# Five of twelve blocks of x transposed by VectorE and GpSimd's transfers, no longer by TensorE

## What is computed

```python
x = x + 0.5 * swiglu(rmsnorm(x, ffn1_norm), ffn1_wg, ffn1_wu, ffn1_wd)   # 2048 -> 5632 -> 2048
x = x + hybrid_mixer(rmsnorm(x, mix_norm), w_in, ..., w_out, cos, sin)   # short convolution and sparse attention
x = x + 0.5 * swiglu(rmsnorm(x, ffn2_norm), ffn2_wg, ffn2_wu, ffn2_wd)
return rmsnorm(x, final_norm)

def rmsnorm(x, g):
    return x * lax.rsqrt(jnp.mean(x * x, axis=-1, keepdims=True) + EPS) * g
```

## Time and profile before

| | |
|---|---|
| median of 3 executions | 1814.29 us |
| span of the profiled execution | 1810.6 us |
| TensorE busy | 1799.3 us, 99% |
| VectorE busy | 1555.0 us, 86% |
| ScalarE busy | 1022.7 us, 56% |
| GpSimd busy | 246.2 us, 14% |
| chain that ended last | PE 93%, DVE 5%, ACT 1%, DMA 1% |

### The profile page before, as it was taken

How to read it: one execution, slowest core, us unless ns; L and a number is a source line. 1 busy time by engine, 2 the same in 40 slices (tenths; PEclk the granted TensorE clock), 3 DMA queues, 4 the chain that set the end, 5 groups by cost and what they waited for, 6 DMA issues and landing times.

```text
span 1810.6 us, 21958 instructions
## 1 busy us (share of the span) xinstructions
PE 1799.3 (99%) x8134; PEld 1481.8 (82%) x8134; DVE 1555.0 (86%) x1863; ACT 1022.7 (56%) x1334; POOL 246.2 (14%) x442
## 2 busy tenths in 40 slices
PE   9999999999999999999999999999999999999998
PEld 7788888888888888888788888888888888888886
DVE  7999998889999977678667867899999889999987
ACT  6655555445555556556567745555555455555554
POOL 1111111001111100000123300111111000222100
PEclk9999999999999999999999999999999999999999
DMA  7676766667676766766443655667676666677764
GB/s 244 209 213 221 217 210 211 207 202 220 206 216 203 218 201 207 209 214 194 149 138 107 209 174 185 209 207 218 209 216 212 214 207 194 209 219 221 242 202 151
DMA packets 199289, 367.28 MB, mean 203 GB/s; under 512 B 19013, under 2 KB 23857, under 8 KB 199057
## 3 DMA queue, kind: packets, MB, share of 16 engines
q1 hardware_dynamic: 185008, 352.37, 62.5%
q0 software_dynamic: 11648, 12.02, 2.2%
q10 hardware_dynamic: 2528, 1.52, 0.3%
HBM read 350.11 MB, written 4.19 MB: 196 GB/s over the span
## 4 chain that ended last, share of the span: by engine, by line
PE 93%; DVE 5%; ACT 1%; DMA 1%; issue 0%; ACTq 0%; DVEq 0%
PE ps L771 23%; PE ps L773 23%; PE ps L772 23%; PE ps L789 7%; PE ps L791 7%; PE ps L790 7%; PE ps L838 2%; DVE w_lo L1820 2%; DVE wt_lo L1892 1%; DVE wt L1882 0%; ACT w_hi L1305 0%; PE ps L1069 0%; PE ps L1096 0%; DMA raw<-in_ffn_wu_dram 0%; PE ps L1071 0%
## 5 line engine op out<-in xcount | busy, mean ns | idle before, releaser
L1820 DVE TENSOR_TENSOR w_lo<-raw,w_hi 128x1024 fp32r<-128x1024 f32 x573 | 692.1, 1225 | 111.8 <-ACT w_hi L1305 107.8
L1305 ACT ACTIVATE w_hi<-raw 128x1024 fp32r<-128x1024 f32 x573 | 599.6, 1056 | 287.3 <-PE ps L773 197.8
L771 PE MATMUL ps<-w_hi,hT_hi 128*128 128x512 f32 x1308 | 512.4, 392 | 1.3 <-ACT gu L1399 1.2
L773 PE MATMUL ps<-w_hi,hT_lo 128*128 128x512 f32 x1308 | 509.6, 390 | 0.0
L772 PE MATMUL ps<-w_lo,hT_hi 128*128 128x512 f32 x1308 | 509.3, 389 | 0.0
L712 POOL DMA_DIRECT2D gu_raw<-gu_sq x352 | 187.5, 541 | 1077.2 <-DVE gu_sq L2066 1003.7
L1356 ACT ACTIVATE wt_hi<-wt 128x1024 fp32r<-128x1024 f32 x164 | 172.9, 1054 | 274.7 <-DVE wt L1882 274.7
L771 PEld LDWEIGHTS ps<-w_hi,hT_hi 128*128 128x128 f32 x1308 | 245.7, 188 | 52.0 <-ACT gu L1399 2.1
L773 PEld LDWEIGHTS ps<-w_hi,hT_lo 128*128 128x128 f32 x1308 | 245.6, 188 | 52.0
L772 PEld LDWEIGHTS ps<-w_lo,hT_hi 128*128 128x128 f32 x1308 | 245.7, 188 | 49.7
L1892 DVE TENSOR_TENSOR wt_lo<-wt,wt_hi 128x1024 fp32r<-128x1024 f32 x164 | 199.6, 1217 | 0.0
(11 more groups left out here) (312 smaller groups left out, 2219.6 us busy)
## 6 DMA issues: line engine op xcount, KB each, us to landing
raw<-in_ffn_wu_dram SPq DMA_DIRECT2D x176, 512.0 KB, 4.5
raw<-in_ffn_wd_dram SPq DMA_DIRECT2D x176, 512.0 KB, 4.8
raw<-in_ffn_wg_dram SPq DMA_DIRECT2D x175, 512.0 KB, 4.1
raw<-in_w_in_dram SPq DMA_DIRECT2D x88, 512.0 KB, 3.6
raw<-in_w_out_dram SPq DMA_DIRECT2D x32, 512.0 KB, 4.2
gu_raw<-gu_sq POOLq DMA_DIRECT2D x352, 32.0 KB, 3.5
x_parked<-x SPq DMA_DIRECT2D x8, 256.0 KB, 5.3
raw<-in_cmp_k_w_dram SPq DMA_DIRECT2D x8, 256.0 KB, 3.2
```

Of the source, the lines that this page charges most:

```text
L771: mm(o, x_hi, w_hi[:, s, kk, :], start=begin, stop=False, skip_group_check=skip)
L773: ins = mm(o, x_lo, w_hi[:, s, kk, :], start=False, stop=last and kk == GK - 1, skip_group_check=skip)
L1305: act.activation(w_hi[:, c % SLOTS, :, :], raw[:, c % SLOTS, :, :], ACT.Copy).then_inc(hi_ready, 1)
L1820: tt(w_lo[:, s, :, :], raw[:, s, :, :], w_hi[:, s, :, :].bitcast(F32), ALU.subtract).then_inc(lo_ready, 1)
```

## The change

Blocks (1, 0), (1, 1), (2, 0), (2, 1) and (2, 2), `CARRIED` in this order, take the squares' path; the other seven stay on TensorE. `x_turn` is DVE's squares of x, `x_blocks` POOL's 16 transfers, `moved_operand` the four scaled copies on ACT and the four on DVE, which now read `gu_raw` in SBUF. Four semaphores are new: `x_squares` (turned), `x_moved` (landed, 256 a block), `x_moved_hi`, `x_moved_lo`. As `gu_sq` is single, DVE's next `x_turn` waits for the last block's landing; as `gu_raw` is single, POOL's next transfers wait for DVE's copies of the last block.

```diff
+def turned_by_pe(which, n):
+    return which == 0 or n == NDC - 1 or which == 1 and n == NDC - 2
+CARRIED = [(which, n) for which in (1, 2) for n in range(NDC) if not turned_by_pe(which, n)]
+CARRY_AT = {0: (23, 27, 28), 1: (28, 32, 33)}
...
+            def x_blocks(which, n):
+                u = CARRIED.index((which, n))
+                pool.wait_ge(x_squares, u + 1)
+                if u:
+                    pool.wait_ge(x_moved_lo, u)
+                for a_ in range(QB):
+                    for c_ in range(QB):
+                        pool.dma_start(gu_raw[c_ * SQ:c_ * SQ + SQ, :, a_, :],
+                                       gu_sq[a_ * SQ:a_ * SQ + SQ, :, c_ * P:c_ * P + P]).then_inc(x_moved, 16)
...
             ffn(0)
+            for n in CARRY_AT:
+                x_blocks(1, n)
...
+            for n in range(NDC - 1):
+                x_blocks(2, n)
             ffn(1)
...
             def x_operand(which, j):
-                pe.wait_ge(free[4 + j % 2], operand_use(which, j % 2, j // 2) + 1)
+                if turned_by_pe(which, j // 2):
+                    pe.wait_ge(free[4 + j % 2], operand_use(which, j % 2, j // 2) + 1)
+                else:
+                    pe.wait_ge(x_moved_lo, CARRIED.index((which, j // 2)) + 1)
...
-                        if f == 0 and part == 1 and g in (X0_AT, len(order) - 1):
-                            x_transposes(1, int(g > X0_AT))
...
-                for n in range(NDC - 1):
-                    put(AT[("out", NDC + n + 1), 1], lambda n=n: x_transposes(2, n))
...
+            def moved_operand(which, n):
+                vec0 = (V_FFN1, V_MIX, V_FFN2)[which]
+                act.wait_ge(x_moved, 16 * QB * QB * (CARRIED.index((which, n)) + 1))
+                for kk in range(QB):
+                    k = QB * n + kk
+                    ins = act.activation(hT_hi[:, k, :].rearrange("p (g s) -> p g s", s=SQ),
+                                         gu_raw[:, :, :, kk * SQ:kk * SQ + SQ].rearrange("p t a s -> p (t a) s"),
+                                         ACT.Copy, scale=vecs[:, vec0 + k:vec0 + k + 1])
+                ins.then_inc(x_moved_hi, 1)
...
-                            if f == 0 and g == X0_AT + 4:
-                                x_operand(1, 0)
+                            for n, steps_ in CARRY_AT.items():
+                                if f == 0 and g == steps_[1]:
+                                    moved_operand(1, n)
...
                 for n in range(NDC - 1):
-                    put(AT[("out", NDC + n + 1), 3], lambda n=n: x_operand(2, n))
+                    if n < NDC - 2:
+                        put(AT[("out", NDC + n + 2), 2], lambda n=n: moved_operand(2, n))
...
+            def x_turn(which, n):
+                u = CARRIED.index((which, n))
+                dve.wait_ge(resid_done, resid((None, R_FFN1B, R_ATT)[which], n))
+                if u:
+                    dve.wait_ge(x_moved, 16 * QB * QB * u)
+                for t in range(NT):
+                    ins = nc.vector.transpose(gu_sq[:, t, :].rearrange("p (c k s) -> p c k s", c=QB, s=SQ),
+                                              x[:, t, n * CH:n * CH + CH].rearrange("p (k c s) -> p c k s", c=QB, s=SQ))
+                ins.then_inc(x_squares, 1)
...
+                    put(done("out", NDC + n) + 1, lambda n=n: x_turn(2, n))
+                    if n < NDC - 2:
+                        put(AT[("out", NDC + n + 2), 3], lambda n=n: moved_operand(2, n))
```

More of the change, by code:

```diff
@@ L156 @@
 R_FFN1B, R_CONV, R_ATT, R_FFN2B = range(4)
+def turned_by_pe(which, n):
+    return which == 0 or n == NDC - 1 or which == 1 and n == NDC - 2
+CARRIED = [(which, n) for which in (1, 2) for n in range(NDC) if not turned_by_pe(which, n)]
+TURNED = [(which, n) for which in range(2) for n in range(NDC) if turned_by_pe(which, n)]
+CARRY_AT = {0: (23, 27, 28), 1: (28, 32, 33)}
 def resid(stage, n):
@@ L278, in mixer_banks @@
     uses += [(("cb", 0), 6), (("cb", 1), 7), (("css",), 6), (("ass",), 7)]
-    first = {4: 2 * NDC, 5: 2 * NDC, 6: 0, 7: 0}
+    first = {4: len(TURNED), 5: len(TURNED), 6: 0, 7: 0}
     seen, table = dict(first), {}
@@ L498, in build_program @@
         gu_moving = sem("gu_moving")
+        x_squares = sem("x_squares")
+        x_moved = sem("x_moved")
+        x_moved_hi = sem("x_moved_hi")
+        x_moved_lo = sem("x_moved_lo")
         gu_moved = sem("gu_moved")
@@ L846, in x_transposes @@
                     pe.wait_ge(resid_done, resid(R_FFN1B if which == 1 else R_ATT, n))
-                    if which == 1 and n < 2:
-                        pe.wait_ge(prod_free, job_no(0, ("down", 1, n)) + 1)
+                    if which == 1:
+                        pe.wait_ge(prod_free, job_no(0, ("down", 1, 1)) + 1)
                 for b in range(2):
@@ L1855, in x_operand, with moved_operand @@
                 for b in range(2) if b is None else (b,):
-                    scaled_operand(hT_hi, hT_lo, 4 * n + 2 * b, vec0, (4 + b,), OP_X[which] + 2 * n + b)
+                    at_ = len(TURNED) if which == 2 else TURNED.index((which, n))
+                    scaled_operand(hT_hi, hT_lo, 4 * n + 2 * b, vec0, (4 + b,), 2 * at_ + b)
+            def x_turn(which, n):
[7 more added lines that the diff above has]
+                ins.then_inc(x_squares, 1)
+            def moved_operand(which, n):
+                vec0 = (V_FFN1, V_MIX, V_FFN2)[which]
+                dve.wait_ge(x_moved_hi, CARRIED.index((which, n)) + 1)
+                for kk in range(QB):
+                    k = QB * n + kk
+                    split = lambda u: u[:, k, :].rearrange("p (g s) -> p g s", s=SQ)
+                    ins = stt(out=split(hT_lo), in0=gu_raw[:, :, :, kk * SQ:kk * SQ + SQ].rearrange("p t a s -> p (t a) s"),
+                              scalar=vecs[:, vec0 + k:vec0 + k + 1], in1=split(hT_hi).bitcast(F32),
+                              op0=ALU.mult, op1=ALU.subtract)
+                ins.then_inc(x_moved_lo, 1)
             def variance(phase, width, ssq_count, cols=NDC):
@@ L1917, in h_sums @@
                 if step == 0:
-                    for b in range(2):
-                        dve.wait_ge(free[4 + b], operand_use(2 if f else 0, b, 1) + 1)
+                    if f:
+                        dve.wait_ge(x_moved_lo, CARRIED.index((2, 1)) + 1)
+                    else:
+                        for b in range(2):
+                            dve.wait_ge(free[4 + b], operand_use(0, b, 1) + 1)
                     pick = lambda buf: buf[:, k0:k0 + 2 * quads, :].rearrange("p (q r) t -> p q r t", q=quads)
@@ L2169, in down @@
                                 residual(1, FFN0[f] + down_slot(1, 1), 1, half)
-                            if f == 0 and g == X0_AT + 4:
-                                x_operand(1, 0)
+                            for n, steps_ in CARRY_AT.items():
+                                if f == 0 and g == steps_[2]:
+                                    moved_operand(1, n)
+                                if f == 0 and g == steps_[0]:
+                                    x_turn(1, n)
                             if f == 1 and g in (23, 25, 39):
```

18 lines of the change are left out of this document (6 added, 12 removed).

## The result

The changed kernel takes 1838.74 us (median; 1837.36 to 1840.3), the kernel before beside it 1814.13 (1812.19 to 1815.16): ratio 1.0137, 95% interval 1.0125 to 1.0149, 24.6 us slower. The spans of the profiled executions differ by 1835.6 - 1810.6 = 25.0 us, and that is what follows explains. (Medians of the kernel before in later comparisons are 1813.5 to 1814.7.)

What follows compares the result with a forecast made beforehand. TensorE's list of matmuls was taken as the bound. Waits of 4.7 + 5.9 + 14.8 = 25.4 less 4.5 saved gave +20.9 on a span of 1810.6, 1831.5; with 3.7 for the runs' median, 1835 us, range 1825 to 1846.

Steps and rivals of the forecast that it cites:

- What is removed, 4.5 us: Five blocks of eight transposes leave TensorE's list, 0.88 to 0.92 us each, 4.5 us in all.
- Squares to last issue, 1.95 + 8.0: Each carried block: POOL's first transfer 1.95 us after the squares begin, the last of 16 issued 8.0 us later.
- The landing: Last transfer's issue to landed: 4.3 us where weight loads run, 3.4 where they run half, 2.1 with none in flight.
- the sum of +15: Total with the skill's landing of about 2.0 us fixed plus 0.1 for size, +15 not +21; short landings' chance 0.18.
- The copies: In each carried block ACT's four copies take 1.55 us and DVE's four 1.65, with no price for reading squares.
- (1, 0), 4.7 us: Stage 1's first block: ACT stands still 5.5 us for the landing, and TensorE waits 2.2, 2.1 and 0.4, together 4.7.
- Stage 2, 14.8: Mixer's end: a loop of DVE's squares, POOL's transfers and copies makes TensorE wait 1.6, 4.4, 5.9 and 2.9, together 14.8.
- Waits of TensorE, 25 us in all: Expected profile: TensorE waits for `wt_lo` and `w_lo`, 25 us, near 676 to 700 and 1092 to 1135.
- TensorE's clock falls: Rival: idling in the new waits lowers TensorE's clock, up to 1.5 us each, +1 to +4, 1836 to 1839; chance 0.06.
- The sum: Whole kernel: waits 25.4 less 4.5 saved, +20.9 us, forecast 1835.
- the rival of long landings: Rival: landings of 4.3 us and more in all five blocks, +26, 1840; chance 0.12.
- Data in time: Other side: the copies find their data in time, TensorE never waits, 1809.8; chance 0.04.

Runs made afterwards that it cites:

- experiment 4: The changed kernel with a second pair of buffers alone, every piece standing where the change put it: 1829.19 us, ratio 1.0088 to the kernel before.
- experiment 5: The changed kernel with the copies placed later and still the single pair of buffers: 1833.57 us, ratio 1.0113 to the kernel before.
- experiment 7: The kernel before, with VectorE's `w_lo` repeated in eight slots far apart so that TensorE waits: 1869.97 us, ratio 1.031.
- experiment 8: The kernel before with `w_lo` repeated in three mixer output slots, 1834.12 us; then unread matmuls filling two of the waits, 1828.94 us.
- experiment 9: The changed kernel with 22 and 18 unread matmuls ahead of slots 7.2 and F2, in stage 2's two long waits: 1839.71 us, ratio 1.0145.
- experiment 3: The changed kernel with later copies and a second pair of buffers, same 80 transfers: 1809.14 us, ratio 0.9973 to the kernel before.
- experiment 10: The changed kernel with only (1, 0), (1, 1), (2, 0) carried, late copies, single pair of buffers: 1811.34 us, ratio 0.9982 to the kernel before.
- experiment 11: Later copies and a second pair of buffers, with (2, 3) carried as a sixth block: 1809.75 us, ratio 0.9972 to the kernel before.

## Why the prediction was right, step by step

- **What is removed, 4.5 us.** Right: with the waits gone five blocks gave 5.1 (3.3 to 6.7 by the interval), three 3.3 (1.6 to 4.9) where 2.7 was expected.
- **Squares to last issue, 1.95 + 8.0.** 1.6 (656.65 - 655.06, and the same at (1, 1) and (2, 0)) and 8.0: a third of a microsecond too long, and that half of the issues took two thirds of stage 1's cost away shows that it is a term of the path.
- **The landing** was the term mis-sized. I took 4.3, 3.4, 4.3, 2.1, 2.1; measured were 4.5, 5.3, 4.4, 2.8, 2.8. At (1, 1) I had argued from SP's waits for VectorE that the loads are held by then, and they were *not* (DMA share 0.58): a landing 1.9 us longer, behind an issue 0.4 sooner, is most of the difference there, 7.7 of lateness instead of 5.9. The short ones are above the Trainium skill's figure of about 2.0 us fixed and the 0.1 for size estimated from it (DMA: Bandwidth & Descriptors, Anatomy of one DMA) as well, even at a DMA share of 0.16 and 0.17; the sum of +15 that went with it was 10 us off. ScalarE's idle times show the same: 5.4, 6.2, 6.0, 9.8 and 10.7 us, where 5.5, 4 to 5, 6, 8 and 9 were written down.
- **The copies.** ScalarE 1.71 for four where I took 1.55, VectorE 1.67 for 1.65.
- **(1, 0), 4.7 us:** 4.7 measured, as 2.4 of waits and 2.3 of slow pace instead of 4.7 of waits.
- **Stage 2, 14.8:** 17.4. The loop is the one described, POOL's blocks 18.5 and 16.9 us apart where 17.8 and 15.7 were worked out; two landings 0.7 longer each make over half of the difference of 2.6; the rest is not split. Cutting it left 7.7 of 17.4, and later copies with it in place made it worse, so it held most of this cost (experiments 4 and 5).
- **Waits of TensorE, 25 us in all:** the lateness came out at 29.8 us, 18.7 of it waits, in the two places that the text said, and 11.1 matmuls at half clock. *TensorE's clock falls* stood as a rival of 1 to 4 us with a chance of 0.06, up to 1.5 us each. It fell behind four of the five groups of waits, and isolated falls cost 1.9 to 2.9 (experiments 7 and 8), up to twice what I read off. What was right was that most is swallowed: experiment 9 shows it for stage 2, experiment 4 for (1, 0), and VectorE's rows speak for it at (1, 1), where no run was made. So these 29.8 us are mostly lateness of VectorE's stream, and 11 of them only look like a matter of the clock. What the clock added at (1, 1) is, by those rows, under 1 us; that was not tested by itself.
- **The sum.** +20.9 said, +24.6 measured, +3.7: the two places came out 1.8 and 2.6 us dearer, and longer landings are the larger part of both. The range held it. So did the band of the rival of the clock (1836 to 1839), and the rival of long landings (1840) was near; both by luck. The clock added little to the time, and two of five landings were short.
- **Data in time**, the other side: it was never a matter of the path but of its place. Experiments 3, 10 and 11 are faster than the kernel before with transfers and copies of the very kind that cost 25 us here.

## What to carry to other kernels

Work that is taken off the bounding engine onto a path of 14 us costs nothing if its consumer stands farther behind its producer than that in *every* in-order stream on the way (15.6 to 19.9 us from squares to copies in experiment 3). Here it cost over six times its gain where the consumer stood 9 us behind in stage 1 and in a loop in stage 2. Work out issue + landing of the last transfer and place the consumer from that, slots later rather than sooner. Before moving a consumer, look whether it also frees a single buffer for the next round: then later is worse, and a second buffer comes first. When a trace shows slow matmuls behind a wait, see what the next operand's engine was doing: if TensorE meets it just as it gets ready, the slow pace costs little or nothing; if the wait stands alone, it costs mostly 2 to 3 us on top.

## What the runs showed of the hardware

- Over the 4 us behind 25 of the 28 unfilled waits of 1.9 us or more in these runs TensorE's granted clock was 0.50 to 0.64, with 6 to 14 matmuls at the slow pace. Behind the other three it was 0.77 (3.06 us) and 1.00 (1.94 and 2.95 us). Where no second wait followed, the excess was 1.9 to 3.1 us, and no larger behind 12.3 us (2.9) than behind 5.5 (3.1). Waits of 1.53 us in two pieces also brought the clock down, while single ones of 1.25, 1.77 and 1.81 did not. The page's clock row, in slices of 46 us, hides nearly all of it.
- The last of 16 transfers of 32 KB inside SBUF landed 2.8 us after its issue at a DMA share of 0.16 to 0.17 and 4.4 to 5.3 at 0.54 to 0.88; the last of 8 no sooner (4.9 and 5.6).
- Kept busy through the wait with matmuls that nobody reads, TensorE kept 1.00 behind it, which gave 5 us back where the waits stood alone and nothing where a loop set the pace.
